# The mixer of a two-block network: its barrier, its sigmoids, its high halves and the order of its tile work

## The reference

```python
y_sb = from_heads(stick_breaking_attention(...)) @ w_sb_o      # 512 -> 1024
y_mla = from_heads(latent_attention(...)) @ w_mla_o            # 512 -> 1024
g = jax.nn.sigmoid(gate_pre + b_gate)
g_sb, g_mla = g[..., :D_MODEL], g[..., D_MODEL:]
out = (g_sb * y_sb + g_mla * y_mla) @ w_out
```

## Time and profile before

| | us |
|---|---|
| time, three runs | 2651.73, 2655.64, 2655.73 |
| median | 2655.64 |
| the profiled execution's own time | 2651.94 |
| its span, first to last instruction | 2650.2 |
| mean granted clock over the span | 0.989 |
| PE busy over the span | 2561.6 |

### The profile page before, as it was taken

One profiled execution on the slowest core, in us unless ns is written; L12 is line 12 of the kernel. 1 busy time (PEld: TensorE's weight loads), 2 busy tenths in 40 slices (PEclk: granted clock), 3 DMA queues, 4 the chain that ended last, 5 costly groups with the idle time before them and its releaser, 6 DMA issues.

```text
span 2650.2 us, 34810 instructions
## 1 busy us (share of the span) xinstructions
PE 2561.6 (97%) x13318; PEld 2116.0 (80%) x13318; DVE 1285.5 (49%) x1395; ACT 932.3 (35%) x1306; POOL 1001.2 (38%) x445
## 2 busy tenths in 40 slices
PE   7999999998999999999999899999999899999999
PEld 7999998956777788888676578888877678888887
DVE  4343104367446434420586766663165755666313
ACT  4222223275333332222444232222254543222223
POOL 4433443302223354444332344444444114444443
PEclk9999999999999999999999999999999999999999
DMA  4222232201112232223221132233222112222321
GB/s 171 87 90 80 82 98 86 82 1 56 54 59 73 70 104 99 94 82 99 84 80 48 57 103 95 96 99 104 98 88 80 33 40 96 95 95 95 107 99 64
DMA packets 65904, 220.28 MB, mean 83 GB/s; under 512 B 8273, under 2 KB 8529, under 8 KB 65682
## 3 DMA queue, kind: packets, MB, share of 16 engines
q1 hardware_dynamic: 63792, 216.99, 25.1%
q10 hardware_dynamic: 2018, 1.99, 0.3%
HBM read 216.31 MB, written 2.10 MB: 82 GB/s over the span
## 4 chain that ended last, share of the span: by engine, by line
PE 86%; DVE 8%; ACT 3%; issue 2%; DVEq 0%; DMA 0%; ACTq 0%; SPq 0%; POOL 0%
PE PS L297 26%; PE PS L299 26%; PE PS L298 26%; PE PS L2698 1%; DVE acc L496 1%; ACT xh L470 1%; PE PS L1251 1%; PE PS L1598 1%; DVE h L566 1%; DVE mt L1776 1%; PE PS L2679 1%; DVE xl L474 1%; PE PS L1236 0%; DVE sq L488 0%; PE PS L2717 0%
## 5 line engine op out<-in xcount | busy, mean ns | idle before, releaser
L292 POOL TENSOR_TENSOR wlo<-wraw,whi 128x1024 fp32r<-128x1024 f32 (+2 forms) x425 | 995.5, 2345 | 1572.3 <-ACT whi L285 1571.9
L297 PE MATMUL PS<-xh,whi 128*128 128x512 f32 (+2 forms) x2536 | 906.5, 357 | 38.7 <-DVE xl L474 20.4
L298 PE MATMUL PS<-xl,whi 128*128 128x512 f32 (+2 forms) x2536 | 894.1, 353 | 0.0
L299 PE MATMUL PS<-xh,wlo 128*128 128x512 f32 (+2 forms) x2536 | 893.8, 352 | 0.0
L285 ACT ACTIVATE whi<-wraw 128x1024 fp32r<-128x1024 f32 (+2 forms) x425 | 429.2, 1011 | 835.5 <-PE PS L299 833.3
L297 PEld LDWEIGHTS PS<-xh,whi 128*128 128x128 f32 (+1 forms) x2536 | 478.5, 189 | 111.0 <-DVE xl L474 24.2
L299 PEld LDWEIGHTS PS<-xh,wlo 128*128 128x128 f32 (+1 forms) x2536 | 479.0, 189 | 65.4 <-issue 0.2
L298 PEld LDWEIGHTS PS<-xl,whi 128*128 128x128 f32 (+1 forms) x2536 | 478.9, 189 | 61.5 <-issue 1.4
L297 PE MATMUL PS<-hid2h,whi 128*128 128x512 f32 x560 | 217.8, 389 | 0.0
L298 PE MATMUL PS<-hid2l,whi 128*128 128x512 f32 x560 | 217.8, 389 | 0.0
L299 PE MATMUL PS<-hid2h,wlo 128*128 128x512 f32 x560 | 217.8, 389 | 0.0
(11 more groups left out here) (401 smaller groups left out, 3194.5 us busy)
## 6 DMA issues: line engine op xcount, KB each, us to landing
wraw<-w_up_dram SPq DMA_DIRECT2D x96, 512.0 KB, 3.3
wraw<-w_dn_dram SPq DMA_DIRECT2D x48, 512.0 KB, 3.3
wraw<-w_f1gu_dram SPq DMA_DIRECT2D x44, 512.0 KB, 3.3
wraw<-w_f2gu_dram SPq DMA_DIRECT2D x44, 512.0 KB, 3.3
wraw<-w_hyin_dram SPq DMA_DIRECT2D x24, 512.0 KB, 3.3
wraw<-w_win_dram SPq DMA_DIRECT2D x18, 512.0 KB, 3.3
wraw<-w_gate_dram SPq DMA_DIRECT2D x16, 512.0 KB, 3.2
wraw<-w_pg_dram SPq DMA_DIRECT2D x16, 512.0 KB, 3.3
```

The lines of the kernel that those rows point to most:

```text
L292: pool.tensor_tensor(wlo[:, s, 0:size], wraw[:, s, 0:size], whi[:, s, 0:size].bitcast(F32), ALU.subtract).then_inc(lo_done.s, 1)
L297: pe.matmul(out_, whi[:, s, a:b], xhi, start=start, stop=False, skip_group_check=True)
L298: pe.matmul(out_, whi[:, s, a:b], xlo, start=False, stop=False, skip_group_check=True)
L299: return pe.matmul(out_, wlo[:, s, a:b], xhi, start=False, stop=stop, skip_group_check=True)
```

## The change

`s_latent` hands its signals on, and `s_mix` takes them in place of its barrier: PE waits, chunk by chunk, only for what frees the PSUM banks and writes the tiles which that chunk needs (`bank_free`), ACT waits for each gate tile. The signals of the mixer get names of their own (`"mx"`), since those of the latent stage may still be in use. ACT makes the sigmoids of tiles 0 and 1, splits chunk 4, makes those of tiles 2 to 4, splits chunk 5, and makes the last three tiles' pairs. The high half of the sum is a copy by ACT (`high`), two after each odd chunk's split, in place of a second addition by DVE. DVE makes the products of tile t + 1 ahead of the low half of tile t, and the sum of tile t + 1 behind it. Chunks 4 to 7 wait for the products of the tiles that held their banks (`a1`, `a2`), where they waited for the sums.

```diff
--- before.py
+++ after.py
@@ -1730,22 +1730,35 @@
                 act.activation(ym[:, 3, 0, :], PS3[:, 6, :], ACT.Copy).then_inc(y_hi.s, 1)
             sp_, pool_ = weights("gate")
             stage(pe, act, dve, pool_, sp_)
-
-
-        def s_mix():
+            return p_done, tc_done, y_hi, y_lo, gate_out
+
+
+        def s_mix(before):
+            p_done, transposed, y_hi, y_lo, gate_out = before
             base = BASE["wo"]
-            a1, a2, mx, mh, ml_ = local("st", a1=DT, a2=DT, mx=DT, hi=DT, lo=DT)
+            a1, a2, mx, mh, ml_ = local("mx", a1=DT, a2=DT, mx=DT, hi=DT, lo=DT)
             opened, = local("open", open=16)
 
             def pe(pe):
-                phase_end(pe, "pe")
+
+                def bank_free(c):
+                    if c < 2:
+                        pe.wait_ge(*p_done(31 + c))
+                    if c == 1:
+                        pe.wait_ge(*y_hi(4))
+                        pe.wait_ge(*y_lo(4))
+                    if c == 2:
+                        pe.wait_ge(*transposed(32))
+                    if c == 3:
+                        pe.wait_ge(*gate_out(16))
                 for c in range(8):
+                    bank_free(c)
                     s, _, g = slot_of(base, c)
                     yh_, yl_ = (ym[:, :, 0, :], ym[:, :, 1, :]) if c % 2 else (ysbh, ysbl)
                     pe.wait_ge(*lo_done(g + 1))
                     if c >= 4:
-                        pe.wait_ge(*mh(c // 2 * 2 - 2))
-                        pe.wait_ge(*mx(c // 2 * 2 - 2))
+                        pe.wait_ge(*a1(c // 2 * 2 - 2))
+                        pe.wait_ge(*a2(c // 2 * 2 - 2))
                     for m in range(2):
                         for kt in range(4):
                             c0 = m * 512 + kt * P
@@ -1754,32 +1767,56 @@
                     ins.then_inc(chunk_used.s, 1)
 
             def act(act):
-                phase_end(act, "act")
                 act.preload_act_table_set("sigmoid_and_others")
-                for t in range(DT):
+
+                def sigmoids(t):
                     for x in (t, 8 + t):
-                        act.activation(gate_tile(x), gate_tile(x), ACT.Sigmoid,
-                                       bias=v_("b_gate", x)).then_inc(opened.s, 1)
+                        act.wait_ge(*gate_out(x + 1))
+                        act.activation(gate_tile(x), gate_tile(x), ACT.Sigmoid, bias=v_("b_gate", x)).then_inc(opened.s, 1)
+
+                def high(t):
+                    act.wait_ge(*mx(t + 1))
+                    act.activation(mixh[:, t, :], mt[:, 2, :], ACT.Copy).then_inc(mh.s, 1)
+                sigmoids(0)
+                sigmoids(1)
                 for c in range(8):
                     split_hi(act, base, c + 4)
+                    if c < 2:
+                        for t in range(3 * c + 2, 3 * c + 5):
+                            sigmoids(t)
+                    if c % 2:
+                        high(c - 1)
+                        high(c)
 
             def dve(dve):
-                phase_end(dve, "dve")
-                for t in range(DT):
+
+                def products(t):
                     b = 4 * (t // 2 % 2) + t % 2
                     dve.wait_ge(*opened(2 * t + 2))
                     dve.wait_ge(*chunk_used(base + 2 * (t // 2) + 2))
+                    if t:
+                        dve.wait_ge(*mx(t))
                     dve.tensor_tensor(mt[:, 0, :], gate_tile(t), PS3[:, b, :], ALU.mult).then_inc(a1.s, 1)
                     dve.tensor_tensor(mt[:, 1, :], gate_tile(8 + t), PS3[:, b + 2, :], ALU.mult).then_inc(a2.s, 1)
+
+                def total(t):
                     dve.wait_ge(*a1(t + 1))
                     dve.wait_ge(*a2(t + 1))
+                    if t:
+                        dve.wait_ge(*ml_(t))
                     dve.tensor_tensor(mt[:, 2, :], mt[:, 0, :], mt[:, 1, :], ALU.add).then_inc(mx.s, 1)
-                    dve.tensor_tensor(mixh[:, t, :], mt[:, 0, :], mt[:, 1, :], ALU.add).then_inc(mh.s, 1)
-                    dve.wait_ge(*mx(t + 1))
+
+                def low(t):
                     dve.wait_ge(*mh(t + 1))
-                    dve.tensor_tensor(mixl[:, t, :], mt[:, 2, :], mixh[:, t, :].bitcast(F32),
-                                      ALU.subtract).then_inc(ml_.s, 1)
-                    dve.wait_ge(*ml_(t + 1))
+                    dve.tensor_tensor(mixl[:, t, :], mt[:, 2, :], mixh[:, t, :].bitcast(F32), ALU.subtract).then_inc(ml_.s, 1)
+                products(0)
+                total(0)
+                for t in range(DT):
+                    if t + 1 < DT:
+                        products(t + 1)
+                    low(t)
+                    if t + 1 < DT:
+                        total(t + 1)
             sp_, pool_ = weights("wo")
             stage(pe, act, dve, pool_, sp_)
             return ml_
@@ -2839,8 +2876,8 @@
         summed = s_post_raw("ffn1_post", TK, 0.5, f, parts, "n2", "mix_pre")
         s_win(summed)
         s_mla_project(s_stick())
-        s_latent()
-        led = s_mix()
+        led = s_latent()
+        led = s_mix(led)
         parts = s_out("wout", (8,), lambda kt, i: (mixh[:, kt, :], mixl[:, kt, :]), T, 4, None, f_mix, led)
         summed = s_post_raw("mix_post", T, 1.0, f_mix, parts, "n3", "ffn2_pre")
         led = s_gate_up("f2gu", "n3", T, summed)
```

## The result

The changed kernel takes 2658.78 us (median), the kernel before 2654.47 in the same comparison: a ratio of 1.0015, interval 1.0010 to 1.0021. It is slower by some 4 us, clear of noise and still within 0.2%. The prediction was 2656.0 with a range of 2650 to 2658, so the time lies 0.8 us outside it. A change within 0.2%, to which the prediction gave 0.90, it is; but the change is +4.3 us where the sum of the likeliest case had +0.36.

The account below looks back on a forecast made before the run. PE, busy for 97% of the span, was taken as the bound; only 4.04 us of its waits could go. A new 4.40 us wait replaced them, so +0.36 on 2655.64 gave 2656.0 us, range 2650 to 2658.

Parts of the forecast that it names:

- the likeliest case: POOL's split holds low half 5, so PE waits 4.40 us before the output projection: +0.36 us, 2656.0; chance 0.50.
- the 4.04 us in four pieces: PE's losses around the mixer: barrier 1.54, chunk 4 1.71, output projection 0.35, tile 8 0.33, plus a 0.11 us restart.
- Steps 1 to 3: Mixer: barrier away -1.54 us; sigmoids between splits 0; chunk 4 waiting for products, not sums, -1.71 and -0.11 us.
- D: Waits of chunks 0 to 3 hold PE as long as the barrier did: +1.9 us, 2657.5; chance 0.05.
- Step 4: Mixer: ACT's high-half copy takes 0.60 us (0.61 to 0.71 as bounds) and isn't what ends last.
- Step 5: Mixer's end: low half 5, behind tile 6's products and POOL's split, opens the output projection at 856.86, a 4.40 us wait.
- B: DVE starts low half 5 before POOL's split, so PE opens the output projection at 854.72: -1.78 us, 2653.9; chance 0.30.
- Compared with 865.48: +0.36: Tile 8 of the output projection's opening comes at 865.84 in place of 865.48, +0.36 us.
- C: Clock falls behind the new stall: A plus 1.6 (cheap end) to 5.1 us (dear end), 2657.6 to 2661.1; chance 0.15.
- A: POOL starts before DVE's low half 5; PE waits 4.40 us before the output projection: +0.36 us, 2656.0; chance 0.50.
- The rest of the kernel moves with it: Behind the output projection's opening the kernel is bound by PE and shifts by the same +0.36 us.
- 2655.64 + 0.36: Whole kernel: the median of three earlier runs, 2655.64 us, plus 0.36 us gives the forecast 2656.0.

Follow-up runs that it names:

- e1: Changed kernel with the low half of odd tiles put ahead of the next tile's products again; median -7.2 us against the kernel before, ratio 0.9972.
- e4: Kernel before with only the mixer's barrier replaced by the change's chunk-by-chunk waits; median -4.1 us against the kernel before, ratio 0.9983.
- e0: The changed kernel run again, nothing altered; median +4.2 us against the kernel before, ratio 1.0016.
- e2: Changed kernel with 18 extra PE matmuls filling the wait between chunk 7 and the output projection; median -0.3 us against the kernel before, ratio 0.9999.
- e6: Kernel before, barrier and both DVE sums kept, with products of tile t+1 ahead of low half t; median +2.1 us against it, ratio 1.0011.
- d5: Kernel before with 5 extra matmuls (1.1 us delay) in the middle of the output projection; median +2.6 us against the kernel before, ratio 1.0003.
- d9: Kernel before with 9 extra matmuls (2.0 us delay) in the middle of the output projection; median +1.2 us against the kernel before, ratio 1.0003.
- e3: Changed kernel with ACT's last weight split of the mixer put behind its last two high halves; median +0.3 us against the kernel before, ratio 1.0000.
- d13: Kernel before with 13 extra matmuls (3.0 us delay) in the middle of the output projection; median +4.9 us against the kernel before, ratio 1.0019.

## Why the prediction was wrong

- *What bounds the kernel, and the 4.04 us in four pieces:* right. e1 has none of these waits, and its mixer is shorter by 4.33 us.
- *Steps 1 to 3* (barrier, sigmoids, chunk 4): right, each start to 0.1 us. The change "does what it says"; D didn't happen. What I had not seen is that the barrier's removal alone gives 3.02 us in the mixer (e4), not 1.54, since DVE's chain falls differently against POOL's splits. In the changed kernel that makes no difference, as chunk 4 doesn't wait at all.
- *Step 4* (high half by ACT): it takes 0.63 us and isn't what ends last, as said.
- *Step 5* (low half 5 behind the products and behind POOL): right in mechanism, place and price. PE opened at 856.79 against 856.86. The margin by which POOL won was 0.07 us, not 0.12; it won in each of the four profiles of that order (changed and e0 by 0.07, e2 by 0.06, e6 by 0.28). B, with its 0.30, happened in none of them.
- *"Compared with 865.48: +0.36":* this is the step that failed, as the sum of the likeliest case. e2, with the clock held up, has +0.20 in the mixer; the changed kernel has +1.50 and +2.43. The term that it put at nothing is C, the clock behind the new stall, which measured 1.3 to 2.2 us. It stood in the prediction as a rival with a chance of 0.15, though the row that I named for it had the clock fall behind a stall of 3.39 us, and A's stall was 4.4. With A taken as likeliest, C should have been part of it: then its cheap end, 2657.6, would have been the forecast. The rows were also too few for the other half of the argument: that stalls of 1.5 and 1.7 us leave the clock at 1.00 held in the profile of the kernel before, and not in d5 and d9.
- *"The rest of the kernel moves with it":* wrong too, by some 2 us for this kernel and by up to 3 either way for others. Here it made the median 2658.8 in place of about 2657, and so put it outside the range. The clock of the later stages differs between executions, and its mean over the runs is lower in this kernel (0.9866 against 0.9877).
- *"2655.64 + 0.36":* the base was the median of three runs; that of 22 is 2654.47. By luck the 1.17 us too much in the base hid part of the miss: the time is 2.8 us over the forecast, the change 3.9 us over it.
- *The range:* it took C's cheap end as its upper bound and left the dear end outside. Both ends of C with A's sum, 2657.6 to 2661.1, hold the measured time, but in part by luck: some 2 us of the change lie behind the mixer, and C's sum has no term for them.

## What to carry to other kernels

Before an operation is moved behind another in an engine's queue, look at what that other one waits for: here low half 5, needed by the next stage's opening, went behind products that wait for the last chunk, and putting it back in front makes 7 us of gain out of 4 of loss. Count the clock in when waits are moved together: behind a stall of 4.2 us in one piece PE ran at 1.2 GHz for 3 to 5 us in each of three profiles, where the same time in four pieces, or the piece filled with matmuls, left it at 2.4 GHz. Pieces are no guarantee, since two profiles have a fall behind 1.47 us. And a low clock costs only where PE sets the pace; where PE waits for its tiles anyway, keeping it busy bought nothing and moved the fall to where it costs; and what a fall costs can vanish in a wait that follows. One profile of each kernel isn't enough for differences of 4 us in 2655: two profiles of one kernel differed by 4.8 us in a stretch that the change doesn't touch.

## What the runs showed of the hardware

- A `wlo` of POOL and a low half of DVE that ask within 0.07 us of each other don't share: the second takes 2.82 us in place of 0.69.
- The clock fell behind a stall of 4.17 us in all three profiles that have one unfilled (for 3.2, 4.9 and some 3 us of work), and not in the one in which it was filled.
- A fall that was prevented at 903 us came at 924.6, behind a stall of only 2.30 us, with shorter ones ahead of it; behind the single stall of 2.0 us in e3 there was none. Behind the barrier's 1.47 us there was one in d5 and d9 and none in the kernel before and d13. So a stall's length alone doesn't decide.
- With a delay of 1.1 us in the middle (d5) the runs of a kernel lay 13 us apart, and their mean granted clocks between 0.985 and 0.991.
- In POOL's stretch of 1319.70 to 1508.14 us, one execution of the changed kernel took 190.83 us at a mean clock of 0.96, another 186.01 at 0.98.
